# Attention scores of a 64-wide head contracted over 128 rows

## The chip, the core and the metric

The kernel runs on one core of a Trainium2 chip. The metric is the device time of one execution in microseconds (us). TensorE is called PE (its weight loads PEld), VectorE DVE, ScalarE ACT, GpSimd POOL, the engine that issues the loads SP.

## What is computed

A decoder layer over 512 tokens of width 1024, all in float32: x passes a SwiGLU feed-forward block (width 2816), a token mixer, a second SwiGLU block and a gated input embedding, each between RMS norms. The change is in the mixer, which has 8 stick-breaking heads and 8 forgetting heads, each of width 64:

```python
def stick_breaking_block(q_blk, k_pre, v_pre, q_start):
    z = einsum('bhqd,bhkd->bhqk', q_blk, k_pre) * (HEAD_DIM ** -0.5)
    causal = s_idx < t_idx
    log_1m_beta = where(causal, log_sigmoid(-z), 0.0)
    tail = cumsum(log_1m_beta, axis=3, reverse=True) - log_1m_beta
    a = where(causal, exp(log_sigmoid(z) + tail), 0.0)
    return einsum('bhqk,bhkd->bhqd', a, v_pre)

def forgetting_block(q_blk, k_pre, v_pre, fcum_q, fcum_k, q_start):
    logits = einsum('bhqd,bhkd->bhqk', q_blk, k_pre) * (HEAD_DIM ** -0.5)
    logits = logits + fcum_q[..., :, None] - fcum_k[..., None, :]
    logits = where(s_idx <= t_idx, logits, -inf)
    return einsum('bhqk,bhkd->bhqd', softmax(logits, axis=-1), v_pre)
```

## The kernel before, in words

Everything is kept transposed: features on the 128 partitions, the 512 tokens along the free dimension. Matrix products use a split of float32 into a high part (type float32r) and a low part (the rest). `product` (L1104 to L1108) issues three matmuls for each product: high stationary times high moving (L1106), low times high (L1107), high times low (L1108). ACT makes the high parts by a copy, DVE the low parts by a subtraction. Each engine has its own instruction stream, written by hand and tied to the others by semaphores, so that the order of the work on an engine is the order of the code.

The stages are `up(0)` and `down(0)` (first feed-forward block), `mixer_start`, four `mixer_tile`s, the output projection, `up(1)` and `down(1)`, and the gated embedding. A mixer tile j holds two stick-breaking heads and two forgetting heads; `hh` is 0 or 1, and hd = 2j + hh counts the passes, 8 in all. In a pass one head of each kind is worked on. The queries and keys of both heads of a tile lie on top of each other, those of hh = 0 on partitions 0 to 63, those of hh = 1 on 64 to 127 (`rows`). `hold` (DVE, L872) keeps the six projected rows q, k, v of both kinds; `qk_split` makes the high parts (ACT, L545) and the low parts (DVE, L877) of the four q and k rows. For tile 0 it runs in `mixer_start`, for tile j + 1 in the pass hh = 1 of tile j, after weight unit 3 (`unit(3)`) and before `out_hi`.

PE's order in one pass is:

- Z scores for four blocks of keys, 512, 384, 128 and 256 columns wide: three 64-row matmuls and one 128-row matmul (L1311), which adds the mask through the identity. Three banks, each signalled by `z_done`.
- the logits of query blocks 3, 2 and 0, 512, 384 and 128 columns: three 64-row matmuls, one 128-row matmul with the forget-gate rows `aug` (L1323), one with the mask (L1324).
- for hh = 0 the four transposes of V of the forgetting head (L1260).
- `project(0)`, a third of the projection of the next tile: 24 matmuls with 512 columns. In the last tile `parts(0)` in its place: 18 matmuls (hh = 0) or 9 (hh = 1) of the output projection.
- 20 matmuls with a triangle and with ones, which make the suffix sums (L1345). They wait for the low halves of softplus (`sp_lo`).
- the logits of block 1 (256 columns), `project(1)` or `parts(1)`.
- `weigh` for the stick-breaking head (12 matmuls, waits for `a_lo`), ten transposes of the softmax (L1376), `project(2)` or `parts(2)`, `weigh` for the forgetting head (waits for `pt_lo`).

The other engines follow. After `z_done` ACT computes abs, exp and ln (L597, L599, L601), DVE the softplus (L951), ACT its high half (L605), DVE its low half (L955). Then come V's halves (L549, L882), the row maxima of the logits (DVE, L961), their exps (ACT, L615), the normalisation (L972, L974) and two weight units: ACT copies the high half of a loaded weight unit (L427), DVE subtracts (L746); the last tile has also copies of the parts (L592, L941). After L1345 ACT takes exp (L624) and the high half (L626), DVE the low half (L985). `out_hi` (L637, L443) and `out_lo` (L1000, L766) take a head's output; L644 and L1008 split the transposed softmax.

SP loads the weight units; no load is touched by the change. POOL sums squares for the norms (`add_squares`, L398) and, at L401 to L403, clears the buffer `wf_r` of the forget-gate weights once the first down projection is finished (`w_used` of `U_MIX`). The arrays live in `big`, 44 rows of 512 columns, which also holds the hidden activations of the feed-forward blocks: high parts in rows 0 to 21, low parts in rows 22 to 43.

Of the kernel before, what the change touches and what calls it, by code (L numbers as in the profile page):

```python
# [24 lines left out]
P = 128  # L25
SEQ = 512
# [5 lines left out]
HD = 64  # L32
# [35 lines left out]
U_DOWN = [u + UP_UNITS for u in U_UP]  # L68
U_MIX = U_DOWN[0] + DOWN_UNITS
# [32 lines left out]
def build(nc, t, out):  # L102
    f32, f32r = mybir.dt.float32, mybir.dt.float32r
    ALU, ACT, AX = mybir.AluOpType, mybir.ActivationFunctionType, mybir.AxisListType.X
    MUL, ADD, SUB, MAX, MIN = ALU.mult, ALU.add, ALU.subtract, ALU.max, ALU.min
# [4 lines left out]
    with ExitStack() as ctx:  # L110
# [3 lines left out]
        def sem(name):  # L114
            return ctx.enter_context(nc.semaphore(name))

        def plain(ap):
            return ap.bitcast(f32)
# [5 lines left out]
        big = sb("big", [P, 2 * FC, SEQ], f32r)  # L124
# [17 lines left out]
        ident_r, tri_r, full_r, mask_sb, mask_fx = (const_r[:, i, :] for i in range(5))  # L142
        H = [big[:, 0:FC, :], big[:, FC:2 * FC, :]]

        qk = {n: [big[:, 2 * i + p, :] for p in range(2)] for i, n in enumerate(["q_sb", "k_sb", "q_fx", "k_fx"])}
        v_r = {n: [big[:, 8 + 2 * i + p, :] for p in range(2)] for i, n in enumerate(["v_sb", "v_fx"])}
        aug = [big[:, 12 + i, :] for i in range(2)]
        wf_r = [big[:, 14:16, :], big[:, 16:18, :]]
        oT = [big[:, 18:26, :], big[:, 26:34, :]]

        wide = big[:, 34:44, :].rearrange("p r n -> p (r n)").rearrange("p (i n) -> p i n", n=Z_COLS)
# [17 lines left out]
        hold = scratch[:, 0:3072].rearrange("p (c n) -> p c n", n=SEQ)  # L169
# [18 lines left out]
        w_hi, w_lo, w_used = sem("w_hi"), sem("w_lo"), sem("w_used")  # L188
# [5 lines left out]
        gate_out, up_out, silu_done, h_f, h_hi_s, h_lo_s = map(sem, (  # L194
            "gate_out", "up_out", "silu_done", "h_full", "h_hi", "h_lo"))
        y_done, y_copied, y_scaled = sem("y_done"), sem("y_copied"), sem("y_scaled")
        wf_zero, wf_hi, wf_lo, f_done, f_step, f_act, f4_ready = map(sem, (
            "wf_zero", "wf_hi", "wf_lo", "f_done", "f_step", "f_act", "f4_ready"))
        hold_ready, qk_hi, qk_lo, v_t, v_hi, v_lo = map(sem, (
            "hold_ready", "qk_hi", "qk_lo", "v_t", "v_hi", "v_lo"))  # L200
# [153 lines left out]
        @block.gpsimd  # L354
        def _(pool):
            n = [0]

            def settle(ins):
                n[0] += 1
                ins.then_inc(zeroed, 1)  # L360

            settle(pool.memset(ident[:, :], 0.0))
            settle(pool.memset(const_in[:, 0, :], 0.0))
            settle(pool.memset(const_in[:, 1, :], -1.0))
            settle(pool.memset(const_in[:, 3, :], 0.0))
            settle(pool.memset(const_in[:, 4, :], 0.0))
            settle(pool.memset(pick[:, :, :], 0.0))
            pool.memset(const_in[:, 2, :], -1.0).then_inc(consts, 1)
            pool.memset(ones[:, :], 1.0).then_inc(consts, 1)
            pool.memset(eps_col[:, :], EPS).then_inc(consts, 1)  # L370
            pool.memset(plain(f4[:, :]), 0.0).then_inc(consts, 1)
            pool.wait_ge(zeroed, n[0])

            def select(m, sign, op, fill, base=0):
                return pool.affine_select(out=m, in_=m, compare_op=op, fill=fill, base=base,
                                          pattern=[[-sign, m.shape[-1]]], channel_multiplier=sign)
            select(ident[:, :], 1, ALU.not_equal, 1.0).then_inc(consts, 1)
            select(const_in[:, 0, :], 1, ALU.not_equal, 1.0).then_inc(consts, 1)
            select(const_in[:, 1, :], 1, ALU.is_ge, 0.0).then_inc(consts, 1)
            select(const_in[:, 3, :], -1, ALU.is_gt, MASKED).then_inc(consts, 1)  # L380
            select(const_in[:, 4, :], 1, ALU.is_ge, MASKED).then_inc(consts, 1)
            for i in range(4):
                if i % 2:
                    pool.wait_ge(consts, 9 + i)
                select(pick[:, i // 2, :], 1, ALU.not_equal, 1.0, base=-32 * i).then_inc(consts, 1)

            def add_squares(n, chunks=DC):

                if n:
                    pool.wait_ge(summed, n)  # L390
                pool.memset(acc[:, 0, :], 0.0).then_inc(acc_zero, 1)
                pool.wait_ge(acc_zero, n + 1)
                for k in range(chunks):
                    at = 8 * n + k
                    pool.wait_ge(squared, at + 1)
                    if at:
                        pool.wait_ge(added, at)
                    pool.tensor_tensor(acc[:, 0, :], acc[:, 0, :], sq[:, k % 2, :], ADD).then_inc(added, 1)  # L398
            add_squares(N_FFN1_PRE)

            pool.wait_ge(w_used, U_MIX)  # L401
            for p in range(2):
                pool.memset(plain(wf_r[p]), 0.0).then_inc(wf_zero, 1)  # L403
            add_squares(N_MIX_PRE)
            add_squares(N_MIX_POST, DC - 2)
            add_squares(N_FFN2_PRE)
            add_squares(N_PLE_PRE)
# [8 lines left out]
        def _(act):  # L416
# [123 lines left out]
            def qk_split(tile, kind):  # L540

                first = isinstance(tile, int) and tile == 0
                act.wait_ge(hold_ready, (2, 4)[kind] if first else 6 * tile + 3 * kind + 2)
                for name, c in ((("q_sb", 0), ("k_sb", 1)), (("q_fx", 3), ("k_fx", 4)))[kind]:
                    act.activation(qk[name][0], hold[:, c, :], ACT.Copy).then_inc(qk_hi, 1)  # L545

            def v_split(tile, kind):
                act.wait_ge(v_t, 2 * tile + kind + 1)
# [193 lines left out]
        def _(dve):  # L742
# [129 lines left out]
                dve.scalar_tensor_tensor(hold[:, c, :], src, scale, rms[:, 0, :], MUL, MUL).then_inc(hold_ready, 1)  # L872

            def qk_split(tile, kind):
                for i, (name, c) in enumerate(((("q_sb", 0), ("k_sb", 1)), (("q_fx", 3), ("k_fx", 4)))[kind]):
                    dve.wait_ge(qk_hi, 4 * tile + (2 * kind + i + 1))
                    dve.tensor_tensor(qk[name][1], hold[:, c, :], plain(qk[name][0]), SUB).then_inc(qk_lo, 1)  # L877

            def v_split(tile, kind):
                name = ("v_sb", "v_fx")[kind]  # L880
# [222 lines left out]
        def _(pe):  # L1103
            def product(dst, w_hi_ap, w_lo_ap, m_hi, m_lo, start, stop):  # L1104

                pe.matmul(dst, w_hi_ap, m_hi, start=start, stop=False, skip_group_check=True)  # L1106
                pe.matmul(dst, w_lo_ap, m_hi, start=False, stop=False, skip_group_check=True)  # L1107
                return pe.matmul(dst, w_hi_ap, m_lo, start=False, stop=stop, skip_group_check=True)  # L1108
# [154 lines left out]
            def mixer_tile(j, more):  # L1263
                for hh in range(2):
                    hd = 2 * j + hh
                    rows = slice(HD * hh, HD * hh + HD)

                    def project(g, halves=(0, 1)):
                        if not more:
# [26 lines left out]
                            last.then_inc(w_used, 1)  # L1296


                    if hh == 0:
                        pe.wait_ge(qk_lo, 4 * j + 2)  # L1300
                    pe.wait_ge(a_exp, 3 * hd + 1)
                    if not more and hh == 1:
                        pe.wait_ge(part_lo, PART_AT[1][0][0])
                    kt, qt = qk["k_sb"], qk["q_sb"]
                    for b in range(3):
                        for c in Z_BANKS[b]:
                            _, at, w = Z_AT[c]
                            dst = Z[b][:, at:at + w]
                            product(dst, kt[0][rows, c * P:(c + 1) * P], kt[1][rows, c * P:(c + 1) * P],
                                    qt[0][rows, c * P:SEQ], qt[1][rows, c * P:SEQ], at == 0, False)  # L1310
                            last = pe.matmul(Z[b][:, at:at + P], ident_r, mask_sb, start=False, stop=True, skip_group_check=True)  # L1311
                        last.then_inc(z_done, 1)
                    if hh == 0:
                        pe.wait_ge(qk_lo, 4 * j + 4)

                    def logits(b):
                        lb, at, w = L_AT[b]
                        lbank = L_BANKS[lb % 2]
                        dst = lbank[:, at:at + w]
                        qf, kf = qk["q_fx"], qk["k_fx"]  # L1320
                        product(dst, qf[0][rows, b * P:(b + 1) * P], qf[1][rows, b * P:(b + 1) * P],
                                kf[0][rows, 0:w], kf[1][rows, 0:w], at == 0, False)
                        pe.matmul(dst, aug[0][:, b * P:(b + 1) * P], aug[1][:, 0:w], start=False, stop=False, skip_group_check=True)  # L1323
                        return pe.matmul(lbank[:, at + b * P:at + (b + 1) * P], ident_r, mask_fx, start=False, stop=True,  # L1324
                                         skip_group_check=True)
# [12 lines left out]
                    for c in range(TB):  # L1338
                        b, at, w = Z_AT[c]
# [29 lines left out]
                    for b in range(3):  # L1369
                        tbank = (T_BANK, L_BANKS[1], L_BANKS[0])[b]  # L1370
                        for c in Z_BANKS[b]:
                            _, at, w = Z_AT[c]
# [18 lines left out]
            rows = GAINS[0][1]  # L1391
# [2 lines left out]
            pe.wait_ge(const_hi, 1)  # L1394
            up(0, 0)
            down(0)
            mixer_start()
            pe.sem_inc(o_done, 1)
            with pe.Fori(0, TILES - 1) as j:
# [44 lines left out]
            for r in range(2 * TB):  # L1444
                half, b = divmod(r, TB)
# [68 lines left out]
```

## Time and profile before

| what | us |
|---|---|
| three runs | 1196.76, 1197.9, 1197.67 |
| their median | 1197.67 |
| span of the profiled execution | 1196.8 |
| busy in it: PE, DVE, ACT, POOL | 1150.8, 635.6, 510.1, 64.9 |
| mixer passes in it, from the first Z score to the last L1345 group | 428.14 to 691.28 |

The profiled execution has no time of its own beside its span; 1196.8 stands at the lowest of the three runs, 0.9 below their median (0.07%). In a timeline row the columns are start, duration, engine, line, operation, output and inputs, with the idle time before it and what ended that in brackets. PE's durations there overlap, since matmuls are pipelined; in the chain of waits each piece counts only the time by which it moved the chain on, so a matmul's step is to be read there. "Granted clock" is TensorE's clock as a share of full speed.

### The profile page before, as it was taken

Reading aid. Unit: us, or ns where it says so; the run is one execution under the profiler, and the core shown is the slowest. Engines: PE = TensorE matmul, PEld = TensorE weight load, DVE = VectorE, ACT = ScalarE, POOL = GpSimd, SP = SyncE. Lnnn points to the kernel's source line nnn. Section 1 sums busy time; section 2 is a strip of 40 time slices with the busy share of each in tenths; the row PEclk is TensorE's granted clock in tenths of the full one; section 3 lists DMA queues with packets and bytes.
Section 4 is the critical chain, followed back from the end, with each engine's and each line's share of the span. In section 5 each row is a group of like instructions: output and inputs, shape, how many; then the busy total and the mean of one; then the engine's idle time right before and its main releaser. Section 6 shows DMA issues by size and latency. Waiting matters only on the chain.

```text
span 1196.8 us, 15572 instructions
## 1 busy us (share of the span) xinstructions
PE 1150.8 (96%) x5066; PEld 938.9 (78%) x5066; DVE 635.6 (53%) x1007; ACT 510.1 (43%) x909; POOL 64.9 (5%) x68
## 2 busy tenths in 40 slices
PE   7999999999997999999999998799999999999897
PEld 6888888888885877888788776588888888888675
DVE  6454454542226865655556658945454454333745
ACT  5433333332224455646556653443333334333536
POOL 5000000000001300000000003400000000000120
PEclk9999999999998988998888899899999999999999
DMA  5233333322222311211111013133333334444001
GB/s 177 89 88 105 96 96 96 98 97 96 96 97 71 80 27 53 54 45 43 35 31 39 27 45 81 48 100 97 96 88 105 96 107 126 139 151 135 1 18 71
DMA packets 99011, 97.02 MB, mean 81 GB/s; under 512 B 7136, under 2 KB 82976, under 8 KB 98976
## 3 DMA queue, kind: packets, MB, share of 16 engines
q1 hardware_dynamic: 98976, 96.56, 27.1%
q8 instruction: 21, 0.34, 0.1%
q14 instruction: 14, 0.11, 0.0%
HBM read 94.44 MB, written 2.10 MB: 81 GB/s over the span
## 4 chain that ended last, share of the span: by engine, by line
PE 88%; DVE 7%; ACT 3%; issue 1%; DMA 0%; DVEq 0%; SPq 0%; ACTq 0%
PE bank L1106 28%; PE bank L1108 27%; PE bank L1107 27%; PE bank L1345 2%; DVE xT L788 2%; PE bank L1323 1%; DVE w_r L746 1%; DVE scratch L1052 1%; DVE xg L772 1%; PE bank L1311 1%; DVE acc L766 1%; ACT xg L459 1%; PE bank L1126 1%; PE bank L1376 1%; DVE scratch L1069 0%
## 5 line engine op out<-in xcount | busy, mean ns | idle before, releaser
L746 DVE TENSOR_TENSOR w_r<-w_raw,w_r 128x512 fp32r<-128x512 f32 x332 | 231.6, 706 | 386.1 <-ACT w_r L427 385.8
L427 ACT ACTIVATE w_r<-w_raw 128x512 fp32r<-128x512 f32 x332 | 206.2, 629 | 448.0 <-PE bank L1108 447.0
L1106 PE MATMUL bank<-xg,w_r 128*128 128x512 f32 x890 | 355.8, 400 | 4.6 <-DVE xg L772 4.6
L1107 PE MATMUL bank<-xg,w_r 128*128 128x512 f32 x890 | 351.5, 395 | 0.0
L1108 PE MATMUL bank<-xg,w_r 128*128 128x512 f32 x890 | 351.0, 394 | 0.0
L1106 PEld LDWEIGHTS bank<-xg,w_r 128*128 128x128 f32 x890 | 171.1, 192 | 42.5 <-DVE xg L772 6.9
L1108 PEld LDWEIGHTS bank<-xg,w_r 128*128 128x128 f32 x890 | 170.2, 191 | 36.4
L1107 PEld LDWEIGHTS bank<-xg,w_r 128*128 128x128 f32 x890 | 170.6, 192 | 35.6 <-issue 0.5
L1106 PE MATMUL bank<-big,w_r 128*128 (+1 forms) x416 | 164.2, 395 | 0.0
L1108 PE MATMUL bank<-big,w_r 128*128 (+1 forms) x416 | 162.9, 392 | 0.0
L1107 PE MATMUL bank<-big,w_r 128*128 (+1 forms) x416 | 162.9, 392 | 0.0
L1106 PEld LDWEIGHTS bank<-big,w_r 128*128 128x128 f32 x416 | 79.0, 190 | 16.6 <-issue 0.2
L1107 PEld LDWEIGHTS bank<-big,w_r 128*128 128x128 f32 x416 | 78.9, 190 | 16.6 <-issue 0.2
L1108 PEld LDWEIGHTS bank<-big,w_r 128*128 128x128 f32 x416 | 78.7, 189 | 16.5
L398 POOL TENSOR_TENSOR acc<-acc,sq 128x512 f32<-128x512 f32 x38 | 56.8, 1494 | 78.1 <-ACT sq L443 61.8
L1106 PE MATMUL bank<-big 64*128 64x128 f32 (+7 forms) x128 | 51.4, 401 | 3.0 <-DVE big L1008 2.2
L1108 PE MATMUL bank<-big 64*128 64x128 f32 (+7 forms) x128 | 45.4, 355 | 0.0
L1107 PE MATMUL bank<-big 64*128 64x128 f32 (+7 forms) x128 | 45.2, 353 | 0.0
L459 ACT ACTIVATE xg<-xT,gains 128x512 fp32r<-128x512 f32 x32 | 23.1, 723 | 45.5 <-DVE xT L788 39.9
L788 DVE TENSOR_TENSOR xT<-xT,scratch 128x512 f32<-128x512 f32 x24 | 39.3, 1639 | 0.1
L483 ACT ACTIVATE big<-scratch 128x512 f32 (+1 forms) x44 | 27.2, 633 | 27.3 <-DVE scratch L821 27.3
L479 ACT ACTIVATE scratch<-scratch 128x512 f32<-128x512 f32 x44 | 27.1, 633 | 27.3 <-DVE scratch L814 27.2
(165 smaller groups left out, 1086.5 us busy)
## 6 DMA issues: line engine op xcount, KB each, us to landing
w_raw<-in_ffn_w_gate SPq DMA_DIRECT2D x88, 256.0 KB, 2.8
w_raw<-in_ffn_w_up SPq DMA_DIRECT2D x88, 256.0 KB, 2.8
w_raw<-in_ffn_w_down SPq DMA_DIRECT2D x88, 256.0 KB, 2.6
w_raw<-in_w_in SPq DMA_DIRECT2D x36, 256.0 KB, 2.8
scratch<-in_w_ple_gate SPq DMA_DIRECT2D x16, 256.0 KB, 3.3
w_raw<-in_w_in SPq DMA_DIRECT2D x24, 128.0 KB, 2.2
scratch<-in_x SPq DMA_DIRECT2D x2, 1024.0 KB, 6.5
w_raw<-in_w_out SPq DMA_DIRECT2D x8, 256.0 KB, 2.7
```

The source lines that it names most:

```text
L398: pool.tensor_tensor(acc[:, 0, :], acc[:, 0, :], sq[:, k % 2, :], ADD).then_inc(added, 1)
L427: act.activation(w_slot(0, slot, 0, 4 * P), w_raw[:, slot, :], ACT.Copy).then_inc(w_hi, 1)
L459: act.activation(xg[:, 0, k, :], xT[:, k, :], ACT.Copy, scale=gains[:, g + k:g + k + 1]).then_inc(xg_hi, 1)
L479: act.activation(gu[a], gu[a], ACT.Silu).then_inc(silu_done, 1)
L483: act.activation(H[0][:, ds(2 * s + a, 1), :], gu[2 + a].unsqueeze(1), ACT.Copy).then_inc(h_hi_s, 1)
L746: dve.tensor_tensor(w_slot(1, slot, 0, 4 * P), w_raw[:, slot, :], plain(w_slot(0, slot, 0, 4 * P)), SUB).then_inc(w_lo, 1)
L766: dve.tensor_tensor(acc[rows, slot, :], acc[rows, slot, :], sq[rows, par, :], ADD).then_inc(added, 1)
L788: dve.tensor_tensor(xT[:, m, :], xT[:, m, :], tmp, ADD).then_inc(x_ready, 1)
L1106: pe.matmul(dst, w_hi_ap, m_hi, start=start, stop=False, skip_group_check=True)
L1107: pe.matmul(dst, w_lo_ap, m_hi, start=False, stop=False, skip_group_check=True)
L1108: return pe.matmul(dst, w_hi_ap, m_lo, start=False, stop=stop, skip_group_check=True)
L1345: last = pe.matmul(Z[b][:, off:off + jw], lhs, sp_r[part][:, 512 * jb + jat:512 * jb + jat + jw], start=False, stop=(jc == TB - 1 and part ...
```

## The change

Two sets of padded copies are added: `k_pad[hh]` holds the stick-breaking keys of head hh on its own 64 partitions and zeros on the other 64, `q_pad[hh]` the same for the queries of the forgetting heads. They are the stationary operands. The moving operands, `q_sb` and `k_fx`, stay the pair of both heads on 128 partitions. A score matmul reads all 128 partitions of both; the zeros take the other head out.

- POOL clears the halves that stay zero once, during the first down projection, after 24 of its 44 weight units are used (`pad_zero`), and then `wf_r`, which moves from rows 14 to 17 to rows 30 to 33 of `big`. Values, `aug` and the padded copies are laid out anew in rows 0 to 17.
- ACT's `qk_split` makes three copies for each kind in place of two: one of 128 partitions and two of 64. DVE's `qk_split` makes three subtractions in place of two. The counts of `qk_hi` and `qk_lo` become 6 a tile.
- PE waits for `qk_lo` in both passes of a tile, and for `pad_zero` ahead of the mixer.

```diff
-        qk = {n: [big[:, 2 * i + p, :] for p in range(2)] for i, n in enumerate(["q_sb", "k_sb", "q_fx", "k_fx"])}
-        v_r = {n: [big[:, 8 + 2 * i + p, :] for p in range(2)] for i, n in enumerate(["v_sb", "v_fx"])}
-        aug = [big[:, 12 + i, :] for i in range(2)]
-        wf_r = [big[:, 14:16, :], big[:, 16:18, :]]
+        halves = [slice(HD * hh, HD * hh + HD) for hh in range(2)]
+        k_pad = [[big[:, 4 * hh + p, :] for p in range(2)] for hh in range(2)]
+        q_pad = [[big[:, 4 * hh + 2 + p, :] for p in range(2)] for hh in range(2)]
+        q_sb = [big[:, 8 + p, :] for p in range(2)]
+        k_fx = [big[:, 10 + p, :] for p in range(2)]
+        v_r = {n: [big[:, 12 + 2 * i + p, :] for p in range(2)] for i, n in enumerate(["v_sb", "v_fx"])}
+        aug = [big[:, 16 + i, :] for i in range(2)]
+        wf_r = [big[:, 30:32, :], big[:, 32:34, :]]
...
-            pool.wait_ge(w_used, U_MIX)
+            pool.wait_ge(w_used, U_DOWN[0] + 24)
+            for hh in range(2):
+                pool.memset(plain(big[halves[1 - hh], 4 * hh:4 * hh + 4, :]), 0.0).then_inc(pad_zero, 1)
+            pool.wait_ge(pad_zero, 2)
             for p in range(2):
                 pool.memset(plain(wf_r[p]), 0.0).then_inc(wf_zero, 1)
...
-                for name, c in ((("q_sb", 0), ("k_sb", 1)), (("q_fx", 3), ("k_fx", 4)))[kind]:
-                    act.activation(qk[name][0], hold[:, c, :], ACT.Copy).then_inc(qk_hi, 1)
+                full, c, pads, cp = ((q_sb, 0, k_pad, 1), (k_fx, 4, q_pad, 3))[kind]
+                act.activation(full[0], hold[:, c, :], ACT.Copy).then_inc(qk_hi, 1)
+                for hh in range(2):
+                    act.activation(pads[hh][0][halves[hh], :], hold[halves[hh], cp, :], ACT.Copy).then_inc(qk_hi, 1)
...
-                for i, (name, c) in enumerate(((("q_sb", 0), ("k_sb", 1)), (("q_fx", 3), ("k_fx", 4)))[kind]):
-                    dve.wait_ge(qk_hi, 4 * tile + (2 * kind + i + 1))
-                    dve.tensor_tensor(qk[name][1], hold[:, c, :], plain(qk[name][0]), SUB).then_inc(qk_lo, 1)
+                full, c, pads, cp = ((q_sb, 0, k_pad, 1), (k_fx, 4, q_pad, 3))[kind]
+                dve.wait_ge(qk_hi, 6 * tile + (3 * kind + 1))
+                dve.tensor_tensor(full[1], hold[:, c, :], plain(full[0]), SUB).then_inc(qk_lo, 1)
+                for hh in range(2):
+                    dve.wait_ge(qk_hi, 6 * tile + (3 * kind + hh + 2))
+                    dve.tensor_tensor(pads[hh][1][halves[hh], :], hold[halves[hh], cp, :], plain(pads[hh][0][halves[hh], :]),
+                                      SUB).then_inc(qk_lo, 1)
...
-                    if hh == 0:
-                        pe.wait_ge(qk_lo, 4 * j + 2)
+                    pe.wait_ge(qk_lo, 6 * j + 2 + hh)
...
-                            product(dst, kt[0][rows, c * P:(c + 1) * P], kt[1][rows, c * P:(c + 1) * P],
-                                    qt[0][rows, c * P:SEQ], qt[1][rows, c * P:SEQ], at == 0, False)
+                            product(dst, kt[0][:, c * P:(c + 1) * P], kt[1][:, c * P:(c + 1) * P],
+                                    q_sb[0][:, c * P:SEQ], q_sb[1][:, c * P:SEQ], at == 0, False)
...
-                    if hh == 0:
-                        pe.wait_ge(qk_lo, 4 * j + 4)
+                    pe.wait_ge(qk_lo, 6 * j + 5 + hh)
...
-                        product(dst, qf[0][rows, b * P:(b + 1) * P], qf[1][rows, b * P:(b + 1) * P],
-                                kf[0][rows, 0:w], kf[1][rows, 0:w], at == 0, False)
+                        product(dst, qf[0][:, b * P:(b + 1) * P], qf[1][:, b * P:(b + 1) * P],
+                                k_fx[0][:, 0:w], k_fx[1][:, 0:w], at == 0, False)
...
+            pe.wait_ge(pad_zero, 2)
             mixer_start()
```

## Rows read from the trace of the kernel before

**Rows 1.** The page, busy us of PE with share and instructions.
```profile
PE 1150.8 (96%) x5066; PEld 938.9 (78%) x5066; DVE 635.6 (53%) x1007; ACT 510.1 (43%) x909; POOL 64.9 (5%) x68
```

**Rows 2.** The page, chain that ended last, shares by engine.
```profile
PE 88%; DVE 7%; ACT 3%; issue 1%; DMA 0%; DVEq 0%; SPq 0%; ACTq 0%
```

**Rows 3.** Windows: stretch, its us, PE busy, granted clock, DMA share, GB/s.
```profile
428.14:445.48 17.34, 17.34 (x59) 0.70 0.16 43
...
502.06:517.89 15.83, 15.83 (x60) 0.78 0.06 17
...
646.84:662.80 15.96, 15.96 (x54) 0.68 0.04 12
677.78:691.28 13.50, 13.50 (x41) 0.62 0.04 10
sum 129.40, PE 129.40; mean PE 16.18
```

**Rows 4.** Windows: between two stretches, the whole of the passes, and two us.
```profile
482.05:502.06 20.01, 20.01 (x113) 1.00 0.26 67
...
428.14:691.28 263.14, 261.48 (x1166) 0.86 0.15 40
...
506.00:508.00 2.00, 2.00 (x7) 0.64 0.00 0
```

**Rows 5.** Chain of waits, head 2: start, us by which the piece moved it, what.
```profile
503.27 0.37 PE bank L1106
503.64 0.17 PE bank L1107
...
503.98 0.26 PE bank L1311
...
518.05 2.70 PE bank L1345 x20
```

**Rows 6.** Chain of waits, head 3: projection (512 columns), then weighing (384, 256, 128).
```profile
563.94 0.23 PE bank L1107
...
564.57 0.17 PE bank L1107
...
565.05 0.12 PE bank L1107
...
565.35 0.11 PE bank L1107
```

**Rows 7.** Timeline of DVE and ACT, head 6 (Z at 646.84), head 7 (677.78).
```profile
653.73 1.63 DVE L955 TENSOR_TENSOR big<-scratch,big 128x512 fp32r<-128x512 f32 x3
...
684.49 1.63 DVE L955 TENSOR_TENSOR big<-scratch,big 128x512 fp32r<-128x512 f32 x3
...
659.62 0.69 ACT L615 ACTIVATE scratch<-bank,stat 128x512 f32<-128x512 f32 x1 [1.35 <-DVE stat L961]
...
661.20 0.60 ACT L592 ACTIVATE xg<-bank 128x512 fp32r<-128x512 f32 x1
...
665.70 0.60 ACT L624 ACTIVATE scratch<-bank 128x512 f32<-128x512 f32 x1 [1.58 <-PE bank L1345]
```

**Rows 8.** Timeline of ACT and DVE, start of the mixer, the splits of tile 0.
```profile
416.56 1.15 ACT L545 ACTIVATE big<-scratch 128x512 fp32r<-128x512 f32 x2 [2.37 <-DVE scratch L872]
...
417.22 1.29 DVE L877 TENSOR_TENSOR big<-scratch,big 128x512 fp32r<-128x512 f32 x2 [0.70 <-ACT big L545]
```

**Rows 9.** Timeline of DVE, ACT and PE, head 1.
```profile
482.25 0.69 DVE L872 SCALAR_TENSOR_TENSOR scratch<-bank,rms 128x512 f32<-128x512 f32 x1 [7.12 <-PE bank L1108]
...
491.95 2.18 ACT L545 ACTIVATE big<-scratch 128x512 fp32r<-128x512 f32 x4
...
497.00 1.62 DVE L1008 TENSOR_TENSOR big<-bank,big 128x512 fp32r<-128x512 f32 x3
...
500.01 0.48 PE L1106 MATMUL bank<-big 128*128 128x512 f32 x1
```

**Rows 10.** Timeline of POOL, the clearing of the forget-gate weights' buffer.
```profile
375.75 1.84 POOL L403 MEMSET big<- 128x1024 f32 x2 [346.34 <-PE bank L1108]
```

More of the change, by code:

```diff
@@ L196, in build @@
         y_done, y_copied, y_scaled = sem("y_done"), sem("y_copied"), sem("y_scaled")
+        pad_zero = sem("pad_zero")
         wf_zero, wf_hi, wf_lo, f_done, f_step, f_act, f4_ready = map(sem, (
@@ L1265, in mixer_tile @@
                     hd = 2 * j + hh
-                    rows = slice(HD * hh, HD * hh + HD)
                     def project(g, halves=(0, 1)):
@@ L1303, in mixer_tile @@
                         pe.wait_ge(part_lo, PART_AT[1][0][0])
-                    kt, qt = qk["k_sb"], qk["q_sb"]
+                    kt = k_pad[hh]
                     for b in range(3):
@@ L1319, in logits @@
                         dst = lbank[:, at:at + w]
-                        qf, kf = qk["q_fx"], qk["k_fx"]
-                        product(dst, qf[0][rows, b * P:(b + 1) * P], qf[1][rows, b * P:(b + 1) * P],
-                                kf[0][rows, 0:w], kf[1][rows, 0:w], at == 0, False)
+                        qf = q_pad[hh]
+                        product(dst, qf[0][:, b * P:(b + 1) * P], qf[1][:, b * P:(b + 1) * P],
+                                k_fx[0][:, 0:w], k_fx[1][:, 0:w], at == 0, False)
                         pe.matmul(dst, aug[0][:, b * P:(b + 1) * P], aug[1][:, 0:w], start=False, stop=False, skip_group_check=True)
```

## The prediction

> **What bounds it now.** The page first: TensorE is busy 96% of the span [rows 1], and the chain of work that ended last is PE for 88% [rows 2]. So PE is the limit wherever the others keep up, and the question is what its score stretches cost. Head h is the one with hd = h (0 to 7), Z(h) the time at which its first score matmul starts, "stretch" the time from Z(h) to its first L1345 matmul: Z scores, logits of blocks 3, 2 and 0, V transposes in even heads, one third of the projection. I cut the trace at these times. The eight stretches take 129.4 us, all of it PE busy, and yet the granted clock is 0.62 to 0.78 [rows 3], which has heads 0, 2, 6, 7 and the sum. From each L1345 to the next Z it is 1.00, by the first of [rows 4], even where 20 short matmuls follow one another. The level is either full or half, 2.4 or 1.2 GHz. The mean of the 263 us from Z(0) to L1345 of head 7 is 0.86, by the second, so 2 x 0.14 x 263 = 74 us ran at half. In head 2 (Z at 502.06) the clock is still whole for 0.56 us after 506 (0.64 over two us, the third): it falls 4.5 us after Z, with PE at work all the time.
>
> The second loss shows in the steps of the chain [rows 5], head 2, still at full clock. Of three products with 384 columns and 64 rows, the second takes 0.17 us and so does the third; the first, coming after a 128-row matmul, takes 0.37. The 128-row mask behind them takes 0.26, where a 128-column matmul among its like takes 0.11 [rows 6]. Going from 128 to 64 rows costs 0.20 us, going back 0.15. The 64 rows themselves save nothing: 384 columns take 0.17 in both forms. A head has 8 blocks, so 16 changes, 128 in all.
>
> **The change, part by part.**
>
> *Switches.* All score products get 128 rows, so the 128 changes go. A head's scores by rows 6 (0.23, 0.17, 0.12, 0.11 for 512, 384, 256, 128 columns): Z is 3 x (0.23 + 0.17 + 0.12 + 0.11) plus 4 masks at 0.11 = 2.33 us. Logits 3, 2, 0: 3 x (0.23 + 0.17 + 0.11), the augmented rows 0.51, masks 0.33 = 2.37. Logits 1 lose two changes, 0.35.
>
> *Clock.* The edit doesn't touch it and no row prices it afterwards. Bounds: it falls as now (gain 0), or never (74 us run at double speed, 37). I take never: each fall begins inside the only stretches that mix 64 and 128 rows, while L1345 and the weighing, short and all 128-row, keep 1.00 [rows 4]; the scores will look like those.
>
> The Trainium skill, "TensorE: Matmul & The Clock Gate" (Part 1), has the clock fall after an idle window. No record here shows PE idle, so by that alone there would be no fall to cure. Its section on a second failure mode lets many small idles do it, and the 0.20 us gaps could be those. By the first reading the falls stay as they are (first rival), by the second they go.
>
> *The new stretches*, at full clock: even heads 2.33 + 2.37 + four transposes 0.44 + 24 x 0.23 = 10.66 us, odd heads 10.22; head 6 (18 matmuls of parts) 9.28, head 7 (9) 6.77. Heads 0 to 5 now: 129.40 - 15.96 - 13.50 = 99.94 [rows 3]; then 3 x 10.66 + 3 x 10.22 = 62.64. Gain 37.3, with 6 x 0.35 = 2.1: 39.4.
>
> *What is late next.* L1345 needs the low softplus halves, which DVE's L955 ends 8.5 us after Z in head 6 (655.36 - 646.84) and 8.3 in head 7 (686.12 - 677.78) [rows 7]. That chain runs on ACT and hardly hangs on the scores. In heads 0 to 5 it leaves 1.7 us in front of 10.2. After L1345 order and work stay, and so do the margins.
>
> Head 6 loses its cover [rows 7]. Softplus low halves at Z + 8.5, V's low half to 9.1, then the three maxima with their exps, which now take 2.3 us after it (L615 0.7 behind the first maximum, 1.58 to L592): 11.4. Two part copies and two weight halves on ACT at 0.55: 13.5. PE would have finished L1345 at 9.28 + 2.70 = 12.0, so L624 starts at 13.5 instead of 18.9 (665.70 - 646.84), and what follows moves with it: gain 5.4. Head 7: PE is ready at 6.8, the softplus at 8.4, against 13.5: gain 5.1, with logits 1 5.4. Both: 10.8, where PE alone would give 14.
>
> *Added copies.* Per tile and kind, three ACT copies and three DVE subtractions replace two of each: 8 more instructions on ACT, 8 on DVE. The added ones cover half the partitions at the same 512 columns. None such is in the trace; those of 128 partitions take 0.57 on ACT and 0.64 on DVE [rows 8], which I charge as the nearest (a lower bound is zero). At the start of the mixer DVE's third subtraction pushes the forget-gate steps by 0.6 us and ACT's copy adds 0.1 at the end: 0.7 once. For later tiles they stand in the odd heads behind the weight splits [rows 9]: ACT's four copies become six (1.1 us), DVE's likewise (1.2). Behind them queue out_hi, then L644 and L1008, for which PE waits before the last weighing. L1008 ends at 498.62 (three from 497.00), PE starts at 500.01: 1.39 us of cover, 0.2 remain, cost nothing. If that cover is gone, 1.2 us in each of heads 1, 3 and 5.
>
> *POOL.* Two clearings of 2,048 columns are new, and those of the forget weights come earlier. Two of 1,024 took 1.84 us [rows 10], so 3.7 us, under the second half of the first down projection; POOL has no part in the chain [rows 2], and nothing but clearings queues behind. Cost nothing; without cover 3.7. No DMA is added or moved. PE gets a wait on copies in each odd head too, made long before: nothing.
>
> **Sum.** 39.4 + 10.8 - 0.7 = 49.5 us off 1196.8: 1147.3. The median of the runs is 0.9 above this span, so 1148.
>
> The skill's "TensorEngine Tiling (Array Packing)" speaks against padding: two products of 64 rows can run side by side in different row groups, up to twice as fast. In rows 5 a head's products come one after the other in one half, and the other head's are over 30 us away, so nothing is forfeited and the sum would be the same.
>
> **Rivals.**
>
> *The clock still falls in every head.* For: nothing idles in rows 3, so something finer brings it down, perhaps rows that do no work, and half of the new stationary is zero. Against: rows 4. Price: on PE, switches and clock together are worth 129.4 - 78.7 + 8 x 0.35 = 53.5 us (78.7: the new stretches summed). Falls as long as now take 37 back, half as long 18, and the copies 0.7: 1162 to 1181, at the length of now 1181. Chance 0.15.
>
> *ACT and DVE become the limit in heads 0 to 5.* For: DVE idles 7.12 us before L872 in head 1 [rows 9], and PE reaches that point 6.8 us sooner, so normalisations, weight halves and L985 close up. Against: it fits, by 0.3 us. A miss of 2 to 3 us a head gives 1160 to 1166. Chance 0.12.
>
> *Slower: the added copies decide.* If the 0.20 us gaps come with the change of operand tile and not of rows (each 64-row triple also changes tile), the scores stay as they are, and what is left is 0.7 us at the start and, where out_hi queues behind the copies in heads 1, 3 and 5, 1.2 each: 1202. It decides once the scores give back less than 0.7 to 4.3 us. Against: L1345 follows the projection, another tile, and its 20 take 2.70 us, none near 0.37 [rows 5]. Chance 0.03; the same with the copies hidden, no change, 0.02.
>
> **How the numbers follow.** The forecast has 0.68. Its low end is 1142: heads 6 and 7 unlimited give 3.4 us more, a start without cost 0.7, rounding of the 0.23 (171 matmuls) about 1. Up to 1174 the second rival and the shorter falls of the first are in; left out are its long falls (0.10), the slower and unchanged cases (0.05) and a little below. A difference under 0.2% (2.4 us) can't be told from none. Faster: 0.68 + 0.15 + 0.12 = 0.95; same 0.02; slower 0.03.
>
> **What would show it.** Right: the first product of each block as short as its second; the mask near 0.11; granted clock 1.00 from 430 to the end of the mixer; stretches of 10.2 to 10.7 us; a wait of PE for L955 in head 7 and for L985 in head 6. Wrong: 0.50 in the clock row (first rival), PE waiting for L955, L985 or L1008 in heads 0 to 5 (second), 0.37 against 0.17 still there (third).

## The result and the profile after

The kernel after takes 1149.92 us (median of 4 runs, 1148.59 to 1151.28) against 1197.79 before (4 runs, one more than in the table above): ratio 0.9597, 95% interval 0.9584 to 0.961. That is 47.9 us less, where 49.5 were forecast. The profiled execution took 1148.77 us with a span of 1147.1; the forecast for the span was 1147.3.

The page of the kernel after, its busy times and the chain of work that ended last, by engine:

```profile
PE 1097.3 (96%) x5066; PEld 911.0 (79%) x5066; DVE 640.0 (56%) x1015; ACT 511.3 (45%) x917; POOL 68.6 (6%) x70
...
PE 85%; DVE 9%; ACT 4%; issue 1%; DMA 0%; DVEq 0%; SPq 0%; ACTq 0%
```

The number of PE instructions is the same as in [rows 1], their busy time is 53.5 us less, and DVE and ACT hold 13% of the chain instead of 10% [rows 2]. The windows of the stretches (from the first Z score of a head to its first suffix-sum matmul, now L1357), in the order of heads 0 to 7 and then the whole of the passes; columns as in [rows 3]:

```profile
427.62:438.66 11.04, 10.97 (x60) 1.00 0.26 71
457.78:468.10 10.32, 10.32 (x58) 1.00 0.11 27
487.80:498.48 10.68, 10.68 (x62) 1.00 0.18 47
...
607.47:616.79 9.32, 9.32 (x56) 1.00 0.12 36
632.91:641.30 8.39, 7.06 (x43) 1.00 0.05 16
427.62:641.30 213.68, 209.21 (x1167) 1.00 0.19 49
```

Here is nearly the whole gain of the profiled executions, whose spans differ by 49.7 us. The granted clock was 0.62 to 0.78 in these stretches [rows 3] and is 1.00 in all of them. The passes went from 263.14 to 213.68 us, 49.5 less; head 2's stretch from 15.83 to 10.68 and head 7's from 13.50 to 8.39. The first steps of head 2 in the chain of waits (L1121 to L1123 are the three matmuls of `product`, L1324 is the mask), and its suffix sums:

```profile
487.96 0.28 PE bank L1121
488.24 0.23 PE bank L1122
488.47 0.23 PE bank L1123
488.70 0.06 PE bank L1324
488.76 0.23 PE bank L1121
488.99 0.18 PE bank L1122
...
489.40 0.11 PE bank L1121
489.51 0.11 PE bank L1122
...
498.64 2.70 PE bank L1357 x20
```

Against [rows 5] the first matmul of the 384-column triple takes 0.23 us where it took 0.37, and the mask 0.06 where it took 0.26. The 0.05 by which that 0.23 is above the 0.18 behind it is the mask's own share, since 0.06 + 0.05 is the 0.11 of [rows 6]. The suffix sums, which the change leaves alone, take 2.70 as before.

What PE waited for within the passes: us in all, times, longest:

```profile
PE bank L1121 <- DVE big L1023: 2.3, 2, 1.2
PE bank L1121 <- DVE big L1000: 1.8, 1, 1.8
...
PE bank L1357 <- DVE big L970: 1.3, 1, 1.3
```

These lie in heads 6 and 7. L1000 is the old L985 and makes PE wait 1.8 us in head 6, where L985 made it wait 0.6; L970 is the old L955 (low halves of softplus) and makes it wait 1.3 us in head 7. L1023, the old L1008, already cost 2.2 us there before. (The 0.2 us for which PE waits at the very first Z score are the same before and after.)

### The profile page after: what moved, and what is told of

Read it like the earlier page. It is cut to its first block, busy times and chain, and to the rows that moved or that the text cites. A ratio compares the mean times of both kernels' runs of the same rounds, so it can differ in the third digit from the quotient of the medians.

```text
span 1147.1 us, 15601 instructions
## 1 busy us (share of the span) xinstructions
PE 1097.3 (96%) x5066; PEld 911.0 (79%) x5066; DVE 640.0 (56%) x1015; ACT 511.3 (45%) x917; POOL 68.6 (6%) x70
## 4 chain that ended last, share of the span: by engine, by line
PE 85%; DVE 9%; ACT 4%; issue 1%; DMA 0%; DVEq 0%; SPq 0%; ACTq 0%
PE bank L1121 27%; PE bank L1123 26%; PE bank L1122 26%; DVE xT L799 2%; PE bank L1357 2%; DVE w_r L757 1%; DVE xg L783 1%; DVE scratch L1067 1%; ACT xg L468 1%; DVE acc L777 1%; PE bank L1141 1%; PE bank L1388 1%; DVE scratch L794 1%; DVE scratch L1084 0%; PE bank L1150 0%
## 5 line engine op out<-in xcount | busy, mean ns | idle before, releaser
L1121 PE MATMUL bank<-xg,w_r 128*128 128x512 f32 x890 | 351.2, 395 | 4.3 <-DVE xg L783 4.2
L1123 PE MATMUL bank<-xg,w_r 128*128 128x512 f32 x890 | 347.8, 391 | 0.0
L1122 PE MATMUL bank<-xg,w_r 128*128 128x512 f32 x890 | 347.7, 391 | 0.0
L1121 PEld LDWEIGHTS bank<-xg,w_r 128*128 128x128 f32 x890 | 168.0, 189 | 42.0 <-DVE xg L783 7.0
L1123 PEld LDWEIGHTS bank<-xg,w_r 128*128 128x128 f32 x890 | 167.9, 189 | 35.6
L1122 PEld LDWEIGHTS bank<-xg,w_r 128*128 128x128 f32 x890 | 168.0, 189 | 34.6 <-issue 0.5
L1121 PE MATMUL bank<-big,w_r 128*128 (+1 forms) x416 | 162.9, 392 | 0.3 <-DVE xg L956 0.3
L1123 PE MATMUL bank<-big,w_r 128*128 (+1 forms) x416 | 161.9, 389 | 0.0
L1121 PEld LDWEIGHTS bank<-big,w_r 128*128 128x128 f32 x416 | 78.1, 188 | 16.5 <-issue 0.6
L1123 PEld LDWEIGHTS bank<-big,w_r 128*128 128x128 f32 x416 | 78.1, 188 | 16.5
L1121 PE MATMUL bank<-big 128*128 128x128 f32 (+3 forms) x128 | 43.6, 340 | 4.3 <-DVE big L1023 2.3
L397 POOL MEMSET acc<- 128x512 f32 x5 | 2.6, 525 | 662.9 <-PE bank L1141 406.1
L1123 PE MATMUL bank<-big 128*128 128x128 f32 (+3 forms) x128 | 41.2, 322 | 0.0
L1122 PE MATMUL bank<-big 128*128 128x128 f32 (+3 forms) x128 | 41.1, 321 | 0.0
```

## The experiments

Two theories were open after the result: the gaps at the changes of row count bring the clock down (A), or work on 64 of 128 rows does (B). In the kernel before they always come together. A "fall" is a stretch of time at half clock. "Time at half clock" is worked out from a run's window over all passes, as twice (1 - granted clock) times its length; before it was 74 us.

### 64 rows without the gaps

```diff
-                            last = pe.matmul(Z[b][:, at:at + P], ident_r, mask_sb, ...)
+                            last = pe.matmul(Z[b][:, at:at + P], ident_r[rows, :], mask_sb[rows, :], ...)
...
-                        pe.matmul(dst, aug[0][:, b * P:(b + 1) * P], aug[1][:, 0:w], ...)
+                        pe.matmul(dst, aug[0][rows, b * P:(b + 1) * P], aug[1][rows, 0:w], ...)
-                        return pe.matmul(lbank[...], ident_r, mask_fx, ...)
+                        return pe.matmul(lbank[...], ident_r[rows, :], mask_fx[rows, :], ...)
```

> Kernel before, with every matmul of the scores on 64 rows: masks and the augmented forget-gate rows are contracted over the head's own 64 partitions only (the other half of the mask and of the augmented rows is left out). Two changes between 64 and 128 rows are left in Z plus logits 3, 2, 0 and two around logits 1, instead of 16 a head. Theory A, the gaps at the changes bring the clock down: clock 1.00 in all eight stretches, 1150 to 1156 us. Theory B, matmuls on 64 rows bring it down because half of the array does no work: clock 0.62 to 0.78 there as before, only the gaps saved, 1178 to 1188 us.

1153.62 us by the median of four executions, ratio 0.9618 (0.9588 to 0.9647). One of the four took 3602.64 us and is left out of the ratio; nothing explains it. The other three took 1151.69, 1151.92 and 1155.32. Windows of head 2's stretch, of head 6's and of all passes:

```profile
487.55:498.44 10.89, 10.89 (x61) 1.00 0.09 24
609.05:620.20 11.15, 11.15 (x55) 0.85 0.06 18
426.79:643.48 216.69, 213.88 (x1166) 0.99 0.18 49
```

Seven of eight stretches are at full clock, with all scores on 64 rows; head 6's has one fall of 3.4 us. Work on 64 rows alone (theory B) therefore doesn't explain the falls of before; and whether this one fall comes of the 64 rows isn't shown, since a second profile of the kernel after has one of the same length in the same head (below). This kernel leaves out half of each mask, so it isn't one to use; the next asks whether a complete kernel can have the gain without padding.

### The same matmuls in an order with fewer changes

```diff
                     for b in range(3):
                         for c in Z_BANKS[b]:
                             ...
                             product(dst, kt[0][rows, ...], ...)
+                    for b in range(3):
+                        for c in Z_BANKS[b]:
+                            _, at, w = Z_AT[c]
                             last = pe.matmul(Z[b][:, at:at + P], ident_r, mask_sb, ...)
                         last.then_inc(z_done, 1)
```

and likewise for logits 3, 2 and 0, the augmented rows with their masks behind the three triples.

> Kernel before, same matmuls, other order: the four 64-row triples of Z first, then their four masks; the triples of logits 3, 2, 0, then their augmented rows and masks. 6 changes of row count a head instead of 16. Theory A (gaps bring the clock down): no or few falls, 1154 to 1164 us, less what ACT loses by getting the first Z bank 1.3 us later. Theory B (64 rows bring it down): falls as before, 10 x 8 x 0.175 = 14 us saved at most, 1183 to 1192 us.

1160.82 us (1160.64 to 1164.86), ratio 0.9689 (0.9664 to 0.9715), inside A's range. This kernel computes everything, with no padding, no clearing and no further copy, and has three quarters of the gain (3.1% against 4.0%; 37 of 47.9 us). The stretches of heads 0 and 2, and all passes:

```profile
426.90:438.13 11.23, 11.23 (x59) 1.00 0.26 68
488.50:502.88 14.38, 14.38 (x61) 0.76 0.07 18
426.90:654.13 227.23, 223.67 (x1167) 0.96 0.17 46
```

Falls are left in heads 2 and 5 (6.8 us each) and 7 (3.4). With 6 changes a head and 64 rows the clock falls sometimes. That holds for every execution and not only for the profiled one: the granted clock over the whole kernel was 0.977 to 0.981 in the four runs of this one and 0.983 to 0.985 in those of the kernel after.

### The gaps with products on 128 rows

```diff
-                            last = pe.matmul(Z[b][:, at:at + P], ident_r, mask_sb, ...)
+                            last = pe.matmul(Z[b][:, at:at + P], ident_r[rows, :], mask_sb[rows, :], ...)
...
-                        return pe.matmul(lbank[...], ident_r, mask_fx, ...)
+                        return pe.matmul(lbank[...], ident_r[rows, :], mask_fx[rows, :], ...)
```

on the kernel after; `rows` is the head's own half of the partitions.

> Kernel after, all products on 128 rows, but the masks contracted over 64 partitions (half of each mask is left out): 16 changes of row count a head as in the kernel before, each with its gap, and only 128-column masks on 64 rows. Price of the gaps by themselves 16 x 8 x 0.175 = 22 us. Theory A: the clock falls again as before, 1190 to 1205 us. Theory B: the clock stays at 1.00, 1170 to 1176 us.

1166.78 us (1165.84 to 1167.02), ratio 0.9726 (0.9707 to 0.9745). That is far from A's 1190 to 1205 and 3 us below B's 1170 to 1176: 16 changes a head are back, but the clock stays up (0.984 to 0.985 over the whole kernel in all four runs). Head 2's steps of the chain (L1325 is the mask), and the windows of head 2's stretch and of all passes:

```profile
494.57 0.25 PE bank L1325
494.82 0.37 PE bank L1121
495.19 0.18 PE bank L1122
```

```profile
493.66:506.61 12.95, 12.95 (x61) 1.00 0.15 39
428.62:659.26 230.64, 228.90 (x1166) 1.00 0.17 46
```

The mask and the triple's first matmul take what they took in [rows 5] to 0.01 us, although now the mask is the one with 64 rows; against the kernel after (0.06 and 0.23) a pair of changes costs 0.33 us here, where it cost 0.35. So this run is the price of the gaps alone: 1166.78 - 1149.92 = 16.9 us for 128 changes, 0.13 each (15 us by the two ratios, 17.0 by the passes of the two profiles). In heads 0 to 5 a pass is 2.3 to 2.6 us longer, 0.16 for each change; in heads 6 and 7 only 1.1 and 0.8, since there the waits shrink in exchange. The remaining 31 us of the result are the clock's. Set beside the run before, with fewer changes and yet falls, it shows that 64 rows count too: at this size neither the gaps nor the 64 rows bring the clock down as before, both together do.

### The copies alone

The kernel after, with `[rows]` put back into the four lines of the score products.

> Kernel after with all its copies, clearings, places and waits, but the score products contracted over the head's own 64 rows. Either theory of the clock: gaps and falls as before, and the copies alone show, 0.7 us by my sum: 1198 to 1199 us; up to 1202 if they delay L1008 in the odd heads. If the padding or the new places were what helped, it would be well under 1190.

1201.66 us over 10 runs, against 1199.20 for the kernel before in the same rounds: ratio 1.002 (1.0008 to 1.0031), so 1 to 3.7 us slower. That is more than my 0.7. In its profile the clock falls in all heads again (0.85 over the passes), the first Z score comes 0.6 us later, the passes of heads 1, 3 and 5 take 37.12 to 37.17 us where the longest before took 37.02, and one more fall of 10.2 us stands in the place of one of 6.8, which is worth 1.7 us. It is the floor of the change: had the clock and the gaps not followed, it would have been this much slower.

### One half of the change at a time

```diff
-                                k_fx[0][:, 0:w], k_fx[1][:, 0:w], at == 0, False)
+                                k_fx[0][rows, 0:w], k_fx[1][rows, 0:w], at == 0, False)
```

(the stationary operands of the logits likewise; for the other run the same in Z). In each run 8 of the 16 changes a head are left.

> Kernel after, but the logits contracted over the head's own 64 rows: Z padded, logits not. Gaps: 8 of 16 changes go, 8 x 1.2 us = 9 to 10 us. Clock: the first runs ruled out either cause alone (64 rows without gaps and gaps with 128 rows both kept it at 1.00), so theory C: it falls where both meet for long enough. The logits alone have both for about 3.4 us. Theory C: fewer or shorter falls than the 75 us of before, 1155 to 1175 us. If the falls stay as many and as long as before, 1187 to 1190; if none is left, 1158 to 1161.

> Kernel after, but Z contracted over the head's own 64 rows: logits padded, Z not. Gaps saved: 6 changes in logits 3, 2, 0 and 2 around logits 1, about 10 us. Theory C: Z alone has gaps and 64 rows for 3.6 us, so fewer or shorter falls than before, 1155 to 1175 us. All falls kept: 1187 to 1190; none left: 1158 to 1161. If the gains of the two halves do not add up to the whole, the clock is a common cost of both.

Z padded: 1159.26 us, ratio 0.968 (0.9661 to 0.9698). Logits padded: 1162.94, ratio 0.9706 (0.9689 to 0.9723). The windows of all passes, first Z padded, then logits padded:

```profile
427.65:650.51 222.86, 220.45 (x1167) 0.99 0.18 47
```

```profile
430.70:656.47 225.77, 223.58 (x1167) 0.98 0.18 47
```

Either half alone saves 38.6 or 34.9 us, together 73.5, where the whole saves 47.9. They share one gain: one fall of 3.4 us is left in the first and three in the second. Once half of the changes are gone, the clock mostly holds, and the other half is worth 9 to 13 us, of which the falls that are left make 1.7 and 5.1; the rest, some 8 us each time, is the gaps.

### More gaps

```diff
+            def gapped(dst, rows, w_hi_ap, w_lo_ap, m_hi, m_lo, start, stop):
+                pe.matmul(dst, w_hi_ap, m_hi, start=start, stop=False, ...)
+                pe.matmul(dst, w_lo_ap[rows, :], m_hi[rows, :], start=False, stop=False, ...)
+                return pe.matmul(dst, w_hi_ap, m_lo, start=False, stop=stop, ...)
```

in place of `product` for all scores (32 changes a head), and for Z alone (24), both with the 64-row masks.

> Kernel after, with the second matmul of each score triple (low times high) on the head's own 64 rows, which leaves the product exact, and the masks contracted over 64 rows (half of each mask left out): 32 changes of row count a head, twice those of before, most matmuls on 128 rows. Gaps by themselves: 24 more than in masks64's 16 cost 0.14 to 0.16 us each, so 16 x 8 x 0.15 = 19 us on top of its 1167: 1186 us with the clock at 1.00. If enough gaps bring the clock down whatever the rows, it falls in every head: 1203 to 1225 us.

> Kernel after with the 64-row second matmul in the Z triples alone and 64-row masks everywhere (half of each mask left out): 24 changes of row count a head, between the 16 of masks64 (no fall) and the 32 of gaps32 (a fall in every head). Gaps by themselves: 8 x 8 x 0.15 = 10 us over masks64's 1167: 1176 to 1179 if the clock stays at 1.00. If its total of gaps, larger than that of the kernel before, is what counts and rows do not, it falls in every head as there: 1205 to 1220. If 64-row work counts too, fewer falls than in the kernel before.

32 changes: 1232.14 us, ratio 1.0292 (1.0272 to 1.0311). The expectation's "24 more" should read 16 more; its sum has 16. 24 changes: 1206.45 (2 runs), ratio 1.0069 (1.0048 to 1.009). The windows of head 2's stretch and of all passes, with 32 and then with 24 changes:

```profile
508.48:529.63 21.15, 21.15 (x61) 0.68 0.09 23
427.55:722.97 295.42, 294.12 (x1167) 0.83 0.13 36
```

```profile
504.75:521.97 17.22, 17.22 (x62) 0.80 0.11 29
429.71:698.94 269.23, 267.52 (x1166) 0.88 0.15 39
```

The clock falls in every head, 100 and 65 us at half in all. Most matmuls here have 128 rows. The 64-row work did grow with the gaps, from 1,024 columns a head in masks64 to 2,304 and 3,584, but both are less than the 3,840 of the run with Z padded, which has 8 changes and one fall of 3.4 us. So it is the number of gaps that brings the clock down here; that it would do so with no 64-row work at all is not shown, since every gap here needs a 64-row matmul.

The 32 changes even went beyond the upper end of their range, because the falls are longer than it allowed: 1225 is 39 us above the 1186 without falls, so 78 us at half clock, and it was 100, which would give 1236. The gaps themselves don't double at half clock: into 64 rows it is 0.30 us (0.62 against 0.32 for 384 columns in the kernel before), where it is 0.20 at full.

### Something else than zeros in the padding

```diff
-                pool.memset(plain(big[halves[1 - hh], 4 * hh:4 * hh + 4, :]), 0.0).then_inc(pad_zero, 1)
+                pool.memset(plain(big[halves[1 - hh], 4 * hh:4 * hh + 4, :]), 0.01).then_inc(pad_zero, 1)
```

> Kernel after, with 0.01 in place of 0 in the halves that should be zero: the other head leaks into the scores, all instructions stay the same. If zeros cost or save TensorE nothing (clock and steps set by rows and gaps): 1148 to 1152 us, clock 1.00 in all stretches. If the zero half was what kept the clock up, or held it down, a difference over 3 us.

1150.11 us (1148.58 to 1151.85), ratio 0.9601 (0.9581 to 0.962), the kernel after within 0.2 us, clock 1.00 over the passes. That half of the stationary operand is zero changes nothing that shows here.

### What is left over in head 6 and at the start

```diff
             hold_pair(0)
-            qk_split(0, 0)
             dve.wait_ge(f_done, 1)
             dve.tensor_tensor(fz, bank[3][0:HEADS, :], rms[0:HEADS, 0, :], MUL).then_inc(f4_ready, 1)
+            qk_split(0, 0)
...
-                                ahead(U_OUT, 0, 0, r)
+                                if x:
+                                    ahead(U_OUT, 0, 0, r)
...
                     softmax_exp(3, 1)
+                    late_units()
```

`late_units` does for `unit(0)` of the last tile the `ahead` left out above; DVE has the same.

> Kernel after with two pieces of the work on ACT and DVE moved, all of it kept. In the last tile the weight halves of unit(0) (two in head 6, one in head 7) come behind the exps after L1345 instead of before: head 6's L624 starts up to 1.1 us earlier. At the start of the mixer DVE takes the first step of the forget gate ahead of the three subtractions of qk_split(0, 0): that step starts 0.9 us earlier. If what was left over in head 6 is ACT's queue and the start is DVE's, 1.5 to 2.0 us less than the kernel after in the same rounds, about 1148. If other waits take their place at once (a_lo on DVE, the PE end of the projection): no difference.

> The kernel after, unchanged, in the same rounds as the one with moved work: 1149 to 1151 us. Its distance to that one is what the moves are worth.

With the moves 1146.96 us (1145.86 to 1148.25), ratio to before 0.9573 (0.9559 to 0.9587); the kernel after in the same rounds 1149.97 (1149.38 to 1151.45), 0.9599 (0.9585 to 0.9613). The difference is 3.0 us, more than the 1.5 to 2.0 expected; the two intervals overlap slightly, the two sets of runs don't. ACT's first exp after the suffix sums in head 6, with Z at 607.47 in the kernel after and at 606.69 with the moves:

```profile
620.89 0.62 ACT L635 ACTIVATE scratch<-bank 128x512 f32<-128x512 f32 x1
```

```profile
619.09 0.62 ACT L641 ACTIVATE scratch<-bank 128x512 f32<-128x512 f32 x1
```

13.42 us after Z became 12.40. Head 6's pass shrank from 25.44 to 24.69 us, and the time from the first forget-gate matmul to the first Z score from 16.5 to 15.9. That is 1.35 us; between the two profiles a further 1.3 us lies behind the mixer, which the moves do not touch. That is scatter: from PE's 3.9 us wait in the norm behind the mixer to the end it is 445.4 us in the profile of the kernel after and 444.1 in this one, and 443.9 to 446.3 in all thirteen profiles. So 1.35 of the 3.0 us are shown to be the moves'. This kernel is faster than the kernel before and the kernel after.

The second profile of the kernel after has a fall that the first has not. The windows of head 6's pass in it, and then in the first:

```profile
609.00:635.58 26.58, 23.90 (x133) 0.94 0.13 38
```

```profile
607.47:632.91 25.44, 22.37 (x133) 1.00 0.14 40
```

It is a fall of 3.4 us that begins 17.7 us after Z, in the pass in which PE waits for L1000 and L1023; that these waits bring it about is not shown. The longer span of the second profile, 1149.7 against 1147.1, is 1.1 us there and 1.6 us ahead of the first Z score.

## Why the prediction was right

*Switches.* Forecast 2.33, 2.37 and 0.59 us for Z, logits 3, 2, 0 and logits 1; in heads 1 to 7 they take 2.35 to 2.36, 2.41 to 2.42 and 0.58 to 0.59. The price of a pair, 0.35, was right, and a 64-row mask pays nearly the same, 0.33. How it splits into 0.20 and 0.15 is less sure: behind a mask a triple's first matmul takes 0.05 more even without a change, so in [rows 5] 0.05 may belong to the other direction. The third rival is settled: the kernel after changes operand tile as often as before and has no gap, so the gap goes with the row count.

*Clock.* "Never" was right for the profiled execution of the kernel after, and nearly so in general (one fall of 3.4 us in its second profile); the first rival fell. This was the largest term, 37 of the 49.5 us, and no row priced it: it was a choice between two bounds. The reason given, "each fall begins inside the only stretches that mix 64 and 128 rows", pointed the right way but took for one cause what the runs show to be two that add up: none in masks64, some in grouped64, all in the kernel before, all again with 24 or 32 changes. The "rows that do no work" of the first rival count, but only together with the gaps. Of the Trainium skill's two readings ("TensorE: Matmul & The Clock Gate"), that of many small idles fits the passes in part: 24 and 32 changes a head bring the clock down in every head without any idle time in the records, but the 16 of masks64 don't, while the 16 of before, with 64-row products, do. An idle window does not explain the falls in the passes, since in the kernel before PE was recorded busy from each head's first Z score through the fall. Outside the passes the traces agree with it: in the kernel after the clock falls at 378.52 and 692.55, around waits of PE of 2.0 and 3.9 us and of 5.5 and 3.9 us.

*Stretches.* Forecast 10.66 and 10.22, found 10.68 and 10.70 (heads 2 and 4) and 10.32; head 6 9.32 (9.28); head 0 11.04, for which see the copies.

*Heads 6 and 7.* The exps of head 6 were to start at Z + 13.5 and start at 13.42; the pass lost 5.5 us (30.94 to 25.44), forecast 5.4. In head 7 L1357 was to start at 8.4 and starts at 8.39. The timelines of ACT in head 6 and of PE in head 7, kernel after, show the wait for the maxima and the one for L970:

```profile
617.32 0.69 ACT L626 ACTIVATE scratch<-bank,stat 128x512 f32<-128x512 f32 x1 [1.58 <-DVE stat L976]
...
641.30 2.99 PE L1357 MATMUL bank<-big,const_r 128*128 128x512 f32 x20 [1.33 <-DVE big L970]
```

L970 itself ends 8.3 to 8.6 us after Z in every head, where L955 ended 8.3 to 8.5 after it, although the scores in front of it got shorter: from head 1 on the chain on ACT starts behind the output of the head before (L648 at Z + 0.41 in head 1), not behind the scores.

*Copies.* At the start 0.6 us were added (15.91 to 16.52 from the first forget-gate matmul to Z of head 0), forecast 0.7. The sum overlooked a second place: in head 0 the augmented rows (DVE L902) now queue behind the added subtractions and end 2.6 us after Z, where they ended at 1.8, and the logits wait for them. The chain of waits of the kernel after shows it:

```profile
429.66 0.55 DVE big L902
...
430.25 0.50 PE bank L1121
```

That is why head 0's stretch is 0.35 us longer than those of heads 2 and 4, so the copies cost about 1.0 us at the start. In the odd heads 0.2 us of cover were to remain; it is 0.06, by the timeline of DVE and PE in head 1 of the kernel after:

```profile
484.15 1.62 DVE L1023 TENSOR_TENSOR big<-bank,big 128x512 fp32r<-128x512 f32 x3
...
485.83 0.50 PE L1121 MATMUL bank<-big 128*128 128x512 f32 x1
```

L1023 ends at 485.77 and PE starts at 485.83, against 498.62 and 500.01 [rows 9]. The cover is used up, and a further copy there can be expected to cost nearly its full time. A 64-partition copy takes as long as one of 128: DVE's two take 1.40 us together, ACT's 1.27. The trace of the kernel before could have told: its L766, a subtraction's kind of instruction (TENSOR_TENSOR) on 64 partitions and 512 columns, takes 0.68 us. The page counts 8 instructions more on each, as forecast, and POOL's timeline has the clearing with its 3.7 us, 50 us before the first down projection ends:

```profile
320.22 3.67 POOL L409 MEMSET big<- 64x2048 f32 x2 [291.94 <-PE bank L1123]
```

*Second rival.* The margin before L1357 is 1.8 to 2.1 us in heads 1 to 5, and from head 1 to head 5 nothing makes PE wait. It did not come.

*From span to time.* This term was wrong. I added 0.9 us to the span for the median, but a span and a time aren't the same measure: the profiled execution's own time is 1.7 above its span, and 1.1 below the median of its kernel. That makes 2.8 in place of 0.9, which is the 1.9 us by which 1148 is short. All later runs of the kernel before have a time 2.1 above their span; by that the profiled one of before, with its span of 1196.8, took about 1198.9 us (an estimate), which is above the median and not at the lowest time.

## What to carry over

Look at the steps of the chain for the first matmul after a change of row count, and at the granted clock of that stretch; a PE that is "busy" for 100% of a window can still run at half clock. Where 64-row and 128-row matmuls alternate, order them in blocks first (three quarters of the gain here, with no copy added), and pad the stationary operand if the copies have cover. And when PE gets faster by a fifth, take the releases of each wait relative to the head's start: what stays put there is the next limit.

## What was not expected

Sixteen gaps a head with 128-row products leave the clock at 1.00, and twenty-four bring it down in every head. Six gaps with 64-row products bring it down in three of eight. Row count and gaps both weigh, and PE's recorded busy time shows neither. What the chip adds up, and where the limit lies between these runs, stays open.
